# Scores and values of a page step side by side, with a fifth page slot

## The reference

```python
k_past = cache_k[a, page_table].reshape(b_s, past_len, N_HEADS, 2, HEAD_DIM)
v_past = cache_v[a, page_table].reshape(b_s, past_len, N_HEADS, V_DIM)
o_s = diff_attend(qs, pos_new, ((k_past, v_past, pos_past), (kn, vn, pos_new)), lam, slopes)
...
s = s - slopes * dist            # only where dist >= 0
p = softmax(concatenate(scores, axis=-1), axis=-1)
a = p[:, :, 0] - lam * p[:, :, 1]
out = sum over segments of a @ v
```

## Time and profile before

| | us |
|---|---|
| median of 3 runs | 3187.7 |
| lowest, highest | 3186.69, 3192.26 |
| profiled execution | 3186.87 |
| its span, first to last instruction | 3185.1 |
| TensorE busy | 3103.1 (97%) |
| DVE busy | 1507.0 (47%) |
| ACT busy | 1065.2 (33%) |

### The profile page before, as it was taken

One profiled execution on the slowest core, in us unless ns is written; L12 is line 12 of the kernel. 1 busy time (PEld: TensorE's weight loads), 2 busy tenths in 40 slices (PEclk: granted clock), 3 DMA queues, 4 the chain that ended last, 5 costly groups with the idle time before them and its releaser, 6 DMA issues.

```text
span 3185.1 us, 59411 instructions
## 1 busy us (share of the span) xinstructions
PE 3103.1 (97%) x25406; PEld 2913.4 (91%) x25406; DVE 1507.0 (47%) x2160; ACT 1065.2 (33%) x1502; POOL 278.3 (9%) x226
## 2 busy tenths in 40 slices
PE   8999999999988899999999999999999999999998
PEld 8987877787766699999999999999999999999998
DVE  4344444444444454444444444447544444445445
ACT  3233333333333433223222323225333233233333
POOL 0022222222210010000000000004000000000002
PEclk9999999999999999999999999999999999999999
DMA  6469999999998545444444444443444444444442
GB/s 199 147 237 366 362 353 359 373 359 359 361 331 310 193 140 167 137 147 141 146 142 137 144 147 134 146 146 102 145 144 148 152 149 150 148 155 148 146 152 94
DMA packets 341938, 637.98 MB, mean 200 GB/s; under 512 B 11528, under 2 KB 257775, under 8 KB 308367
## 3 DMA queue, kind: packets, MB, share of 16 engines
q1 hardware_dynamic: 337120, 620.67, 55.9%
q0 software_dynamic: 3328, 11.24, 1.0%
q10 hardware_dynamic: 1230, 2.29, 0.2%
HBM read 625.37 MB, written 9.23 MB: 199 GB/s over the span
## 4 chain that ended last, share of the span: by engine, by line
PE 88%; DVE 5%; ACT 3%; issue 2%; DMA 2%; SPq 0%; POOL 0%; ACTq 0%; DVEq 0%; POOLq 0%
PE ps L1688 71%; PE ps L1804 7%; PE ps L1852 3%; PE ps L1829 3%; DVE halves L1121 1%; ACT halves L815 1%; DMA raw<-in_cache_k_dram 1%; PE ps L1957 1%; DVE pa_n L1414 1%; PE ps L1937 1%; PE ps L2100 0%; DVE pa_s L1408 0%; ACT pa_s L953 0%; DMA io_tm<-in_x_sample_dram 0%; PE ps L1842 0%
## 5 line engine op out<-in xcount | busy, mean ns | idle before, releaser
L1121 DVE TENSOR_TENSOR halves<-raw,halves 128x2048 fp32r<-128x2048 f32 x300 | 687.9, 2293 | 667.3 <-ACT halves L815 667.2
L1688 PE MATMUL ps<-xhi,halves 128*128 128x320 f32 (+1 forms) x3840 | 861.7, 311 | 4.6 <-DVE halves L1121 2.4
L815 ACT ACTIVATE halves<-raw 128x2048 fp32r<-128x2048 f32 x300 | 573.4, 1911 | 867.9 <-PE ps L1688 860.8
L1688 PE MATMUL ps<-yhi,halves 128*128 128x336 f32 x2816 | 657.2, 318 | 0.1
L1688 PEld LDWEIGHTS ps<-xhi,halves 128*128 128x128 f32 x3840 | 649.9, 188 | 6.0 <-issue 4.8
L1688 PE MATMUL ps<-xlo,halves 128*128 128x320 f32 (+1 forms) x1920 | 598.2, 312 | 0.0
L1688 PEld LDWEIGHTS ps<-yhi,halves 128*128 128x128 f32 x2816 | 483.1, 188 | 0.5 <-issue 0.4
L1688 PE MATMUL ps<-ylo,halves 128*128 128x336 f32 x1408 | 447.2, 318 | 0.0
L1308 DVE TENSOR_SCALAR keyT<-ps 128x512 f32<-128x512 f32 x256 | 177.0, 692 | 463.4 <-PE ps L1804 463.4
L1688 PE MATMUL ps<-hA_hi,halves 128*128 128x336 f32 (+1 forms) x1408 | 375.6, 314 | 2.9 <-DVE hT L1579 2.8
L1688 PE MATMUL ps<-hB_hi,halves 128*128 128x336 f32 (+1 forms) x1408 | 372.8, 312 | 0.0
(11 more groups left out here) (224 smaller groups left out, 3076.0 us busy)
## 6 DMA issues: line engine op xcount, KB each, us to landing
raw<-in_w_gate_up_dram SPq DMA_DIRECT2D x176, 1024.0 KB, 5.1
raw<-in_cache_k_dram SPq DMA_DIRECT2D x124, 1024.0 KB, 6.8
raw<-in_cache_v_dram SPq DMA_DIRECT2D x121, 1024.0 KB, 8.3
raw<-in_w_down_dram SPq DMA_DIRECT2D x88, 1024.0 KB, 5.0
kv_raw<-in_w_qkv_dram SPq DMA_DIRECT2D x64, 512.0 KB, 8.4
raw<-in_w_qkv_dram SPq DMA_DIRECT2D x16, 1024.0 KB, 5.1
raw<-in_w_o_dram SPq DMA_DIRECT2D x16, 1024.0 KB, 5.4
page<-in_cache_v_dram SPq DMA_DIRECT2D x7, 1024.0 KB, 7.2
```

What stands on the lines that cost most here:

```text
L815: act.activation(whi[t][:, :], raw[r][:, :], ACT.Copy).then_inc(hi_ready[t], 1)
L1121: dve.tensor_tensor(wlo[t][:, :], raw[r][:, :], whi[t][:, :].bitcast(F32), ALU.subtract)\
L1688: mm = pe.matmul(out, l, r, start=first and n == 0, stop=last and n == 2)
```

## The change

Scores and values of a step now stand next to each other, at the end of a step: values of the older page first, then the step's own scores. Both key octets of a page fall into its own step, with one projection chunk (or `turn_block`) and the tile's transposes between them; the other chunk stands behind the tile's matmuls. One `keyT` buffer is left, and its place becomes a fifth page slot. The orders of ACT and DVE follow. The loop ends two steps behind the last page: the last group's probabilities are turned into four places of the bank at once. The work on the new keys starts one step earlier, joins and return transposes two; the new probabilities are turned into another bank; the five loads of x rows are asked for in five steps of GpSimd's program.

The diff, cut to its core, with the unchanged calls of a step named in words where they set the order:

```diff
-SLOTS = 6
+SLOTS = 7
 GROUP = 4
 TURN_LAG, VALUE_LAG = 5, 6
-STEPS = PAGES + VALUE_LAG
+STEPS = PAGES + 2
+def turned_in(t):
+    first = [v for v in (t - TURN_LAG,) if 0 <= v < PAGES - GROUP]
+    return first + (list(range(PAGES - GROUP, PAGES)) if t == STEPS - 1 else [])
+def valued_in(t):
+    if t < PAGES:
+        return [v for v in (t - VALUE_LAG,) if v >= 0]
+    return [PAGES - VALUE_LAG, PAGES - VALUE_LAG + 1] if t == PAGES else list(range(PAGES - GROUP, PAGES))
-NEW_AT = {114 + n: n for n in range(NB)}
-PAIR_AT = {124 + 2 * p: p for p in range(3)}
-HX0 = 124
+NEW_AT = {113 + n: n for n in range(NB)}
+PAIR_AT = {122 + 2 * p: p for p in range(3)}
+HX0 = 122
+BACK_AT = (113, 114, 115, 116, 118)
...
         page_order():
-    order = [("k", n) for n in range(4)] + [("w", n) for n in range(3, 11)]
+    order = [("k", n) for n in range(4)] + [("w", n) for n in range(3, 11)] + [("k", 4)]
     for t in range(STEPS):
-        if 4 <= t + 1 < PAGES:
-            order.append(("k", t + 1))
-        if 0 <= t - VALUE_LAG:
-            order.append(("v", t - VALUE_LAG))
+        if 5 <= t < PAGES:
+            order.append(("k", t))
+        order.extend(("v", v) for v in valued_in(t))
...
         placement:
+        page4 = place("page4", [P, UNIT], F32, z); z += UNIT * 4      (where keyT1 was)
+        pages = raw + [page4] + late
-        keyT = [place("keyT0", [P, UNIT], F32, z), keyT1]; z += UNIT * 4
+        keyT = place("keyT", [P, UNIT], F32, z); z += UNIT * 4
...
         GpSimd, per step t:
-                if t == KV_STEPS * (H - 1) + 1:   (five row loads)
+                if t in BACK_AT:
+                    row_back(BACK_AT.index(t))
...
         keys_out(t, g), on ACT and on DVE:
-                if t >= 2:
-                    wait_ge(s_full, t - 1)
+                if t:
+                    wait_ge(s_full, t)
...
         ACT, per step:
+                if t < PAGES: keys_out(t, 0)
+                if t - 1 in NEW_AT: new_exps(NEW_AT[t - 1])
+                if t in KV_END: kv_rows(KV_END[t])
                 tile_squares (phase 4)
+                if t < PAGES: keys_out(t, 2)
                 tile_turned (phase 3); tile_features (phase 5)
+                probs_out(v) for v in turned_in(t) if v < PAGES - GROUP
+                new_probs_out; then kv_split_hi(n) where KV_FIRST[n - 1] == t
                 out_features; back_features; exps (every fourth step)
+                probs_out of the last group; tile_exps (phase 1); out_squares
...
         DVE, per step:
+                if t in KV_END: kv_features(KV_END[t])
+                if t < PAGES: keys_out(t, 1)
+                queries of the new keys; if t in KV_END: kv_rows(KV_END[t])
                 tile_normed (phase 5); out_means
+                if t < PAGES: keys_out(t, 3)
+                new_sums; tile_means; out_normed; add_sums; queries; tile_bias (phase 1); tile_join (phase 2)
+                factors; back_features; add_values
+                if t < PAGES: scores_out(t); maxima(t // GROUP) in every fourth step
+                new_scores_out; new_values
...
         TensorE, per step:
-            for t in range(-1, STEPS):
-                if t + 1 < PAGES:
-                    turn_keys(t + 1, 0)
-                if 0 <= t < PAGES:
-                    scores(t)
+            for t in range(STEPS):
+                work = list(KV_AT.get(t, ()))
+                if t < PAGES:
+                    turn_keys(t, 0)
+                if t in KV_END:
+                    turn_block(KV_END[t])
+                elif work:
+                    project(*work.pop(0))
                 tile_back (phase 5); tile_turn (phase 3); turn_back
-                if t + 1 < PAGES:
-                    turn_keys(t + 1, 1)
-                if t in KV_END:
-                    turn_block(KV_END[t])
-                if t - VALUE_LAG >= 0:
-                    values(t - VALUE_LAG)
+                if t < PAGES:
+                    turn_keys(t, 1)
+                turn_probs(v) for v in turned_in(t) if v < PAGES - GROUP
                 turn_new_probs; turn_out; join_halves; tile_scores (phase 0); tile_values (phase 3)
+                second turn_back
+                for block, cc in work:
+                    project(block, cc)
+                if t < PAGES:
+                    for v in valued_in(t):
+                        values(v)
+                    scores(t)
+                behind the last page: turn_probs of the last group, then values
+                if t - 1 in NEW_AT: new_values(NEW_AT[t - 1])
+                if t in NEW_AT: new_scores(NEW_AT[t])
```

More of the change, by code:

```diff
@@ L120, in page_slots @@
 def page_slots():
-    last, turns, out = {i: None for i in range(4)}, {i: 0 for i in range(SLOTS)}, []
+    last, turns, out = {i: None for i in range(5)}, {i: 0 for i in range(SLOTS)}, []
     for n in range(len(IN_STEPS)):
         if n == MORE_FROM:
-            last.update({4: None, 5: None})
+            last.update({5: None, 6: None})
         slot = min(last, key=lambda i: -1 if last[i] is None else last[i])
@@ L313, in trunk @@
         aT_new = place("aT_new", [P, 2, 144], F32, hT_at)
-        pages = raw + [place(f"page{i}", [P, UNIT], F32, x_at + 3 * D * 4 + i * UNIT * 4) for i in range(2)]
+        late = [place(f"page{5 + i}", [P, UNIT], F32, x_at + 3 * D * 4 + i * UNIT * 4) for i in range(2)]
         assert 3 * D * 4 + 2 * UNIT * 4 <= 2 * DC * T * 4
@@ L983, in _ @@
             act.wait_ge(cleared, 5)
-            for t in range(-1, STEPS):
-                if t + 1 < PAGES:
-                    keys_out(t + 1, 0)
+            for t in range(STEPS):
+                if t < PAGES:
+                    keys_out(t, 0)
+                if t - 1 in NEW_AT:
+                    new_exps(NEW_AT[t - 1])
+                if t in KV_END:
+                    kv_rows(KV_END[t])
                 if tile_at(t, 4) is not None:
                     tile_squares(tile_at(t, 4))
-                if t + 1 < PAGES:
-                    keys_out(t + 1, 2)
-                if t in KV_END:
[L992 to L995, removed]
+                if t < PAGES:
+                    keys_out(t, 2)
                 if tile_at(t, 3) is not None:
@@ L999, in _ @@
                     tile_features(tile_at(t, 5))
+                for v in turned_in(t):
+                    if v < PAGES - GROUP:
+                        probs_out(v)
+                if t - 1 in NEW_AT:
+                    new_probs_out(NEW_AT[t - 1])
+                for n in range(9, 4 * KV_BLOCKS):
+                    if KV_FIRST[n - 1] == t:
+                        kv_split_hi(n)
                 if t - 2 in PAIR_AT:
@@ L1005, in _ @@
                     exps(t // GROUP - 1)
[L1006 to L1010, removed]
+                for v in turned_in(t):
+                    if v >= PAGES - GROUP:
+                        probs_out(v)
                 if tile_at(t, 1) is not None:
@@ L1443, in _ @@
             dve.wait_ge(cleared, 5)
-            for t in range(-1, STEPS):
-                if t + 1 < PAGES:
-                    keys_out(t + 1, 1)
+            for t in range(STEPS):
+                if t in KV_END:
+                    kv_features(KV_END[t])
+                if t < PAGES:
+                    keys_out(t, 1)
+                if t in NEW_AT:
+                    if NEW_AT[t]:
+                        dve.wait_ge(n_full, NEW_AT[t])
+                    queries(NEW_SEQ[NEW_AT[t]], 2, qn_set)
+                if t in KV_END:
+                    kv_rows(KV_END[t])
                 if tile_at(t, 5) is not None:
                     tile_normed(tile_at(t, 5))
-                if t in KV_END:
-                    kv_features(KV_END[t])
                 if t - 1 in PAIR_AT:
                     out_means(PAIR_AT[t - 1])
-                if t + 1 < PAGES:
-                    keys_out(t + 1, 3)
-                if 0 <= t < PAGES:
[L1456 to L1460, removed]
+                if t < PAGES:
+                    keys_out(t, 3)
+                if t - 1 in NEW_AT:
+                    new_sums(NEW_AT[t - 1])
                 if tile_at(t, 4) is not None:
@@ L1821, in scores @@
                     pe.wait_ge(s_out, t)
[L1822 to L1826 removed]
+                if 0 <= t - TURN_LAG < PAGES - GROUP:
+                    pe.wait_ge(pt_out, t - TURN_LAG + 1)
                 for b, a, j in score_strips():
```

127 lines of the change are left out of this document (63 added, 64 removed).

## The result

The changed kernel takes 3214.6 us in the median of 7 executions (3200.26 to 3219.8), the kernel before 3189.62 (3186.69 to 3192.95): a ratio of 1.0071 [1.006, 1.0081] (not the quotient of the two medians, which is 1.0078), slower by 0.7%. The forecast was 3190, with a range up to 3212: the time lies above both. The profiled execution is one of 3214.6 us, 27.7 above that of before. The executions fall into two kinds: four at a granted clock of 0.989 or 0.990 (3214.6 to 3219.8), three at 0.993 to 0.995 (3200.26 to 3207.13).

What follows compares the result with a forecast made beforehand. The prediction took TensorE to bound the page loop, with DMA close behind. Its terms were 3186.9 - 31 (strips) + 54 (waits) - 1 (start) - 17 (tail) = 3192, forecast as about 3190, range 3170 to 3212.

Steps and rivals of the forecast that it cites:

- The strips: Page loop: 32-column scores directly behind values save 0.29 us per step in 106 steps, -31 us.
- the KV_END waits: Page loop: turn_block waits 1.32 us for kv_features on DVE, 14 times, 18.5 us.
- the tile waits that lost their cover: Page loop: tile_values and tile_scores, no longer behind projection chunks, wait for ACT's copies; 13.2 and 8 us.
- the late exponentials: Page loop: tile_exps end late behind POOL's subtraction, so the second octet waits 1.02 or 0.78 us; 12.6 us.
- the fifth slot: Page loop: a fifth page slot is worth nothing, since the loop waits for no DMA and gets no faster.
- the drawn waits: Page loop: all new TensorE waits drawn from the new engine orders, 67 us; net +54 without today's.
- today's waits: Page loop: TensorE's waits in the kernel before, 1.85 us per head, 13 us, go away.
- the start: Up to scores(0): one step of projection more done and half a key page less, -1 us.
- rival (d): Page loop: two waits of a t = 16h step bring half clock, 3.5 us seven times, total 3214; chance 0.04.
- The tail: -17: Scores(112) to first W_o matmul, parts split at key octet 117 and scores(127): 17 us less, between -27 and +3.
- rival (b): Tail: page and row transfers keep it long, clock falls at waits for k(115) to k(117); 3206, chance 0.14.
- a faster TensorE meets the DMA 4% further on: Page loop: DMA engines are busy 0.96 of a head, so they bound any TensorE gain soon.

Runs made afterwards that it cites:

- e_apart: The changed kernel with a projection chunk put between values and scores of a step; 3239.53 us, 1.0151 against the kernel before.
- f2_all: The changed kernel with late DVE and ACT producers reordered, tile matmuls behind the chunk, e_joins, e_rows and the mixer's pause filled; 3113.42 us, 0.9767 against the kernel before.
- e_joins: The changed kernel with the tail's join factors made a step earlier on DVE and turn_out behind scores; 3191.69 us, 1.0022 against the kernel before.
- e_rows: The changed kernel with the five x row loads asked for in steps 116 to 120; 3204.54 us, 1.0047 against the kernel before.
- b_shift: The kernel before with 16 identity transposes (1.75 us) added in its first SwiGLU block; 3196.18 us, 1.003 against the kernel before.

## Why the prediction was wrong

*Right:* the loop, in the terms that runs test. The strips (-31 forecast; 28.3 by e_apart, which reaches 81 of the 106 steps), the KV_END waits (18.5 and 18.2), the tile waits that lost their cover (21.2 and 23.7), the late exponentials (14 waits; the two steps of a head that have them are 1.00 and 0.77 us longer than in f2_all, drawn as 1.02 and 0.78), a head of 109.7, the fifth slot at nothing in the loop. The sums agree as well: the drawn waits are 67 us, and f2_all, which has none of them, is 71.1 us shorter there than the changed kernel, 67.9 without the clock's 3.2; against before it is 44.4 shorter, where the strips, today's waits and the start make 45 (31 + 13 + 1).

Scores(112) was forecast at 946 and came at 949.5; 3.2 of that is rival (d) in part, half clock in two of the seven steps with two waits. I had taken the waits to leave the clock alone.

*Wrong, the step "The tail: -17":* it measured -8.5. Its second part was mis-sized (78, measured 82.5): I drew the joins with one wait of 3.4 us, and three joins wait 6.6 and three `turn_out` 4.5, with half clock behind one. e_joins, which takes these waits off, gives 70.5. The first part (28, measured 31.6) is rival (b) in small, a wait of 2.9 for k(115) and the half clock around it; e_rows gives 26.7. The third (12.5, measured 14.5) has half clock as well (0.81). (Rival (b) counts 13 us for the first two parts, where the sum has 7 and 5.)

*Wrong, a term that the sum did not have:* everything behind W_o was taken over from before. It is 9.5 us longer, by the band matmuls at half clock (TensorE busy 25.2 us there, in place of 15.3), in the executions that make the median. Rival (d) looked for the clock's price in the loop alone. With 8.5, 3.2 and 9.5 the 3192 of the sum becomes 3213; measured 3214.6. That rival (d) has 3214 as well is chance: of its 24.5 us in the loop 3.2 were there. The three executions at the higher clock (3200.26 to 3207.13) lie in the range, and above the forecast by the tail and the loop's clock.

Two signs named in advance failed with the tail: full clock up to k(117) (0.94), and 12 to 14 us to the last values (14.5). Of the sign in the loop, a DMA share below 0.95, the whole way has 0.94, the head shown 0.96.

The rule weighed there, of the Trainium skill ("TensorE: Matmul & The Clock Gate", Part 1), was the better guide: single pauses of 2.1 to 3 us and pairs of 1.2 and 1.1 us did cost clock in mixer, tail and loop, in some places and executions. The rows that I preferred were of one execution, in which waits up to 2.1 us had left the clock at 1.00; in b_shift it fell behind a pause of 2.09 us. The page also says that the gate's observation does not begin anew with a kernel and varies between runs; the split of b_shift's executions agrees.

*Wrong, though it cost nothing here:* "a faster TensorE meets the DMA 4% further on". f2_all's loop is 6% shorter than before's, at a share of 0.98.

## What to carry to other kernels

When steps are reordered to bring two kinds of matmul together, draw the new order on every engine: here the gain of some 30 us was real and was paid back by producers left in their old places, most of them repaired by moving a line. Cost idle pieces start to start, and look for pauses like the 2 us ahead of the mixer even where nothing is changed, because a shift of the program can change how often the clock drops behind them. Fill such a pause, or move work into it.

## What the runs showed of the hardware that I had not expected

The DMA share does not measure what is left: 0.96 at 361 GB/s, 0.99 at 385 GB/s in f2_all, without one wait for a page. The Trainium skill ("Perfetto Trace Analysis", Identifying the Most-Contended Engine) advises against occupancy for the 16 DMA engines, and these numbers agree.

TensorE's busy time holds the price of changing between strips and full-array work. From scores(0) to scores(112) it is 715.8 us in the changed kernel and 751.4 in e_apart, for the same matmuls. In f2_all it is 694.9, and in the kernel before, for nearly the same matmuls, 34 us more, which no row shows as idle:

```profile
183.40:923.70 740.30, 729.23 (x8856) 585.62 (x8858) 316.67 (x718) 282.09 (x682) 171.19 (x123) 1.00 0.94 354
```
